# One sparse-attention stage in place of two: projection and compression merged, in 64x64 tiles, with the rope swap by SBUF transfers and all pages read by SyncE

## What is computed

```python
def nsa_project(h, w_in, pos):                       # h: 520 tokens x 1024
    z = h @ w_in                                     # 16 heads of q, six k/v groups of 4 x 64, gates
    ...
    return q, rope(q, pos), kc, vc, rope(ks, pos), vs, rope(kw, pos), vw, gates

def nsa_compress(k, pe, w):                          # blocks of 32 rows -> one row
    blk = k.reshape(B, L // L_CMP, L_CMP, NSA_KV, NSA_DH) + pe[:, None, :]
    return jnp.einsum('bclgd,lde->bcge', blk, w)

def nsa_compressed_select(q, kc, vc, pe, wc, qpos):
    kcmp = nsa_compress(kc, pe[0], wc[0])
    vcmp = nsa_compress(vc, pe[1], wc[1])
    ...
    s = jnp.einsum('btgjd,bcgd->bgjtc', qg, kcmp.astype(jnp.float32))   # scores of the compressed keys
    ...                                              # softmax, o_c, and by top_k the selected blocks
```

## Time and profile before

| | |
|---|---|
| time, median of 3 runs (lowest to highest) | 3682.13 us (3681.27 to 3682.18) |
| the profiled execution's own time | 3677.41 us |
| its span, mean granted TensorE clock | 3675.8 us, 0.943 |
| busy share: PE, DVE, ACT, POOL | 88%, 51%, 34%, 11% |
| sparse attention of layer 0, first projection matmul to first matmul of `nsa_attend` | 282.86 us |
| the same in layer 3 | 282.09 us |

### The profile page before, as it was taken

One profiled execution on the slowest core, in us unless ns is written; L12 is line 12 of the kernel. 1 busy time (PEld: TensorE's weight loads), 2 busy tenths in 40 slices (PEclk: granted clock), 3 DMA queues, 4 the chain that ended last, 5 costly groups with the idle time before them and its releaser, 6 DMA issues. The chain is left out here.

```text
span 3675.8 us, 65936 instructions
## 1 busy us (share of the span) xinstructions
PE 3239.0 (88%) x25906; PEld 2993.7 (81%) x25906; DVE 1870.1 (51%) x3122; ACT 1262.5 (34%) x2150; POOL 396.0 (11%) x313
## 2 busy tenths in 40 slices
PE   6966888999889787878999898999989768889997
PEld 6764568999889787758999887999976745789997
DVE  4113654636479745345636484645451136446363
ACT  2103553423245332124323383423231035434232
POOL 2111211000034100020000131000031112100000
PEclk9978999999999899789999998999999889999999
DMA  3163513222222000123222323222232644032222
GB/s 133 70 219 115 159 38 131 86 98 83 77 64 83 19 0 0 63 80 143 89 95 77 92 79 110 92 89 96 63 106 98 192 131 156 30 131 83 92 86 66
DMA packets 136924, 341.21 MB, mean 93 GB/s; under 512 B 42856, under 2 KB 89576, under 8 KB 122488
## 3 DMA queue, kind: packets, MB, share of 16 engines
q1 hardware_dynamic: 112376, 279.25, 23.4%
q0 software_dynamic: 10496, 46.15, 3.7%
q10 hardware_dynamic: 13824, 12.59, 1.1%
HBM read 322.60 MB, written 32.12 MB: 96 GB/s over the span
## 5 line engine op out<-in xcount | busy, mean ns | idle before, releaser
L354 PE MATMUL ffn_ps<-ffn_x_hi_sb,ffn_w_hi_sb 128*128 128x260 f32 x2816 | 572.0, 284 | 40.3 <-DVE ffn_x_lo_sb L165 37.1
L354 PE MATMUL ffn_ps<-ffn_x_hi_sb,ffn_w_lo_sb 128*128 128x260 f32 x2816 | 570.0, 284 | 0.0
L354 PE MATMUL ffn_ps<-ffn_x_lo_sb,ffn_w_hi_sb 128*128 128x260 f32 x2816 | 569.5, 284 | 0.0
L354 PEld LDWEIGHTS ffn_ps<-ffn_x_hi_sb,ffn_w_hi_sb 128*128 128x128 f32 x2816 | 437.1, 190 | 44.9 <-issue 35.8
L354 PEld LDWEIGHTS ffn_ps<-ffn_x_hi_sb,ffn_w_lo_sb 128*128 128x128 f32 x2816 | 437.0, 190 | 0.0
L354 PEld LDWEIGHTS ffn_ps<-ffn_x_lo_sb,ffn_w_hi_sb 128*128 128x128 f32 x2816 | 436.0, 190 | 0.0
L394 ACT ACTIVATE ffn_w_hi_sb<-ffn_raw_sb 128x2048 fp32r<-128x2048 f32 (+2 forms) x152 | 256.8, 1689 | 349.0 <-PE ffn_ps L354 349.0
L446 DVE TENSOR_TENSOR ffn_w_lo_sb<-ffn_raw_sb,ffn_w_hi_sb 128x2048 fp32r<-128x2048 f32 (+2 forms) x152 | 304.8, 2005 | 47.3 <-ACT ffn_w_hi_sb L394 47.3
L412 ACT ACTIVATE ffn_pre_sb<-ffn_ps 128x520 f32<-128x520 f32 x176 | 106.5, 605 | 605.8 <-PE ffn_ps L354 317.1
L461 DVE SCALAR_TENSOR_TENSOR ffn_conv_sb<-ffn_pre_sb,ffn_conv_w_sb,ffn_conv_sb 128x512 f32<-128x512 f32 x176 | 132.3, 752 | 345.1 <-ACT ffn_conv_sb L414 345.1
L354 PE MATMUL ffn_ps<-ffn_inner_hi_sb,ffn_w_hi_sb 128*128 128x260 f32 x1408 | 283.9, 283 | 6.5 <-DVE ffn_inner_lo_sb L479 3.4
(11 more groups left out here) (446 smaller groups left out, 6276.4 us busy)
## 6 DMA issues: line engine op xcount, KB each, us to landing
ffn_raw_sb<-ffn_w_in SPq DMA_DIRECT2D x88, 1024.0 KB, 4.9
ffn_raw_sb<-ffn_w_out SPq DMA_DIRECT2D x32, 768.0 KB, 4.2
nsae_ring_sb<-sel_pages SPq DMA_DIRECT2D x160, 128.0 KB, 2.2
ffn_raw_sb<-ffn_w_out SPq DMA_DIRECT2D x32, 640.0 KB, 3.9
nsap_w_raw_sb<-nsa_w_in SPq DMA_DIRECT2D x32, 512.0 KB, 3.7
gdnp_w_raw_sb<-gdn_w_in SPq DMA_DIRECT2D x32, 512.0 KB, 3.7
nsac_pages_sb<-cmp_pages ACTq DMA_DIRECT2D x96, 128.0 KB, 3.7
nsac_pages_sb<-cmp_pages SPq DMA_DIRECT2D x96, 128.0 KB, 3.6
```

Source lines behind the costliest of these rows:

```text
L354: mm = pe.matmul(psf[:, bank + h, 0:H], wp[:, w[0], w[1]:w[1] + P], xp[:, h * H:(h + 1) * H], start=start and k == 0, stop=stop and k == 2)
```

## The change

`nsa_project` and `nsa_compress` become one stage, `nsa_base` (buffers `nsab_`). Its parts:

- The 16 projection units are the same, in the order 8 to 15, 0 to 7.
- The rope swap is done by DMA: for each of the 12 turned units ACT issues four transfers of 8 partitions from SBUF to SBUF.
- The values and gates are projected in the split form: two passes of 280 columns, each eight steps (`v_step`) of 15 matmuls. Their weights pass through the same ring, which has two raw buffers in place of three.
- The compression is done in nine calls (the prompt, then each sample): 128 plain fp32 matmuls of 64x64 weights with 64 moving columns (40 for the prompt), over the four quadrants of the array; row group g2 writes PSUM bank 6+g2. The calls stand between projection units, and two of them between steps of the values.
- SP alone reads the pages, whole (256 KB, keys and values), four page numbers at a time; 64 transfers a layer.
- The prompt's scores are formed with the compressed keys as 32-column weights in four column tiles, and transposed afterwards.
- The 32 loads for `nsa_attend` are issued by SP after the last call; page numbers are read four at a time there too. Two stores of results are waited for at the end of `nsa_attend` in place of here.

```diff
-        w = Weights(sc, KT * P, 3, 2)
+        w = Weights(sc, KT * P, 2, 2)
...
-            def swap(r):
-                i = rotate[r]
-                pe.wait_ge(copied, i + 1)
...
-                for h in range(2):
-                    mm = pe.matmul(ps[:, 6 + h, 0:H], g.rope_swap, raw(i)[:, h * H:(h + 1) * H], start=True, stop=True)
...
-                    pe.matmul(ps[0:m, 2 * (i % 3), :], x, w_v[:, kt, 0:512], start=(kt == 0), stop=(kt == KT - 1))
-                    mm = pe.matmul(ps[0:m, 2 * (i % 3) + 1, 0:48], x, w_v[:, kt, 512:560], start=(kt == 0),
...
-                        mm = pe.matmul(ps[:, 1 + u % 2, gp * 256:gp * 256 + cols], w[:, kv, l, :], rhs,
-                                       start=(l == 0), stop=(l == 31))
...
+    order = [8, 9, 10, 11, 12, 13, 14, 15, 0, 1, 2, 3, 4, 5, 6, 7]
+    first_turn = 4
+    sample_after = {4: 0, 6: 1, 8: 2, 10: 3, 12: 4, 14: 5}
+    pages_after = {1: (0, 0), 2: (0, 1), 3: (1, 0), 4: (1, 1), 8: (2, 0), 9: (2, 1), 10: (3, 0), 11: (3, 1),
...
+                if b >= 2 and half == 0:
+                    sp.wait_ge(compressed, b)
...
+                _, ids = nc.values_load_multi_w_load_instructions(v.table[0:1, at:at + 4], engines=(sp.engine,),
...
+                if u in pages_after:
+                    pages(*pages_after[u])
...
+            sp.wait_ge(compressed, 9)
             for k in range(2):
-                sample_loads(sp, d, v, j, table, k, range(4), v.kv_in)
+                sample_loads(nc, sp, d, v, j, k, range(4), v.kv_in)
+            sp.wait_ge(v_copied, 10)
...
+                for l in range(32):
+                    for kv in range(2):
+                        for g2 in range(2):
+                            rows = slice(64 * g2, 64 * g2 + 64)
+                            to = 64 * (g2 if kv == 0 else 1 - g2)
+                            mm = pe.matmul(ps[to:to + 64, 6 + g2, 0:cols], w_cmp[rows, kv, l, :], views[rows, kv, l],
+                                           start=(l == 0), stop=(l == 31))
...
+                for tt in range(5):
+                    if kt == 0:
+                        pe.wait_ge(*((copied, 16) if p == 0 else (v_copied, tt + 1)))
...
+                    pe.matmul(out, x_hi[:, x], w_hi, start=(kt == 0), stop=False)
+                    pe.matmul(out, x_hi[:, x], w_lo, start=False, stop=False)
+                    mm = pe.matmul(out, x_lo[:, x], w_hi, start=False, stop=(kt == KT - 1))
...
+            v_step(0, 0)
+            c_scores(0)
+            v_step(0, 1), v_step(0, 2)
+            c_scores(1)
+            v_step(0, 3)
+            c_tokens(0)
+            v_step(0, 4)
+            compress_sample(6)
+            c_tokens(1)
+            for kt in range(5, KT):
+                v_step(0, kt)
+            for kt in range(0, 3):
+                v_step(1, kt)
+            compress_sample(7)
...
+                for base in (0, 64):
+                    for k in range(2):
+                        here, there = base + 8 * k, base + 8 - 8 * k
+                        act.dma_start(swap[here:here + 8, r % 2, :], raw(i)[there:there + 8, :]).then_inc(swapped[r % 2], 16)
```

More of the change, by code:

```diff
@@ new lines, in is_window, with landed, sample_loads @@
+def is_window(k):
+    return k % 6 >= 4
+def landed(k, pool):
+    loads = [m for m in range(k % 2, k + 1, 2) if m >= 2 or not pool]
+    return sum(16 * (1 if is_window(m) else 4) * (4 if m < 2 else 2) for m in loads)
+def sample_loads(nc, eng, d, v, j, k, strips, kv_in):
+    c, h, vals = k % 6 // 2, k % 2, k // 6
+    for l in strips:
+        slot = v.ring[:, k % 2 * 4 + l, :]
+        if is_window(k):
+            eng.dma_start(slot, d["win_state"][j, 4 * h + l, :, vals * 1024:(vals + 1) * 1024]).then_inc(kv_in[k % 2], 16)
+            continue
+        at = (4 * h + l) * PAGES + 4 * c
+        _, pages = nc.values_load_multi_w_load_instructions(v.table[0:1, at:at + 4], engines=(eng.engine,),
+                                                            min_val=0, max_val=N_PHYS - 1)
+        for p, page in enumerate(pages):
+            eng.dma_start(slot[:, p * 256:(p + 1) * 256],
+                          flat(d["sel_pages"][j, bass.ds(page, 1), :, vals * 256:(vals + 1) * 256]
+                               .rearrange("o p n -> p o n"))).then_inc(kv_in[k % 2], 16)
@@ L1522, in nsa_project @@
-        added = sc.sem("added")
+        swapped = [sc.sem(f"swapped{x}") for x in range(2)]
+        parted = sc.sem("parted")
         rotated = sc.sem("rotated")
[L1524 to L1545, removed]
@@ L1585, in _ @@
[L1585 to L1603, removed]
@@ L1605, in _ @@
[L1605 to L1624, removed]
@@ L1627, in nsa_compress @@
[L1627 to L1657, removed]
@@ L1665, in nsa_compress @@
+        c_masked = sc.sem("c_masked")
         c_shifted = sc.sem("c_shifted")
@@ L1680, in nsa_compress, with raw @@
         dve_own = sc.sem("dve_own")
+        stored = sc.sem("stored")
         block = ctx.enter_context(nc.Block())
[L1683 to L1695 removed]
+        def raw(i):
+            return v.qu[:, i, :] if i < 8 else (kv_c if i < 12 else v.kv)[:, i % 4, :]
@@ L1834, in _ @@
+            for x in (x_hi, x_lo):
+                ins = pool.memset(x[:, KT * N:].bitcast(F32), 0.0)
+            ins.then_inc(padded, 1)
+            w.rest(pool, 0)
+            pool.wait_ge(norm.summed, KT)
+            pool.memset(swap_flat, 0.0).then_inc(zeroed, 1)
+            for u in range(1, 22):
+                w.rest(pool, u)
         @block.vector
@@ L1904, in _ @@
             own.settle()
+            dve.wait_ge(v_copied, 5)
             for i in range(NCH):
```

675 lines of the change are left out of this document (397 added, 278 removed).

## The result

| | us, median (lowest to highest) |
|---|---|
| before, 4 runs | 3681.7 (3680.45 to 3682.18) |
| the change, 4 runs | 3560.26 (3557.67 to 3565.68) |

The ratio is 0.9673, with a 95% interval of 0.9656 to 0.9689: 121 us less. The forecast was 3517, 165 less, in a range of 3485 to 3600. The sign and the range held; the time lies outside the main case (3485 to 3545), and a quarter of the forecast gain is missing. The profiled execution of the change is the slowest of the four: 3565.68, span 3564.0, clock 0.945.

What follows compares the result with a forecast made beforehand. TensorE, busy 88% of the span, was taken as the bound, with two gaps (54 us a layer). Terms summed to 199.9 us against 282.86 and 282.09, saving 165.2 over two layers: 3517 us, range 3485 to 3600.

Steps and rivals of the forecast that it cites:

- main case: Whole kernel: the summed terms hold within their bounds, 3485 to 3545 us, chance 0.60.
- Tiles share a round: Compression calls: four quadrants of 64 columns run together, 58 ns a round, 3.7 us a call as lower bound.
- The swap's price: Projection: a rope swap costs TensorE 0.86 us; eleven leave the window, 103.60 to 94.1, a unit staying 5.77.
- The page gap: Before the compression: TensorE's 31.54 us standstill for a cached page goes, leaving pages at 0.
- The stall before the scores: Before the prompt's scores: TensorE newly waits 5.5 us for keys that VectorE makes after the last unit's rotation.
- the second pass of the values: Values: the second pass waits 2.4 us while ACT loads a function table and copies out the first's results.
- SP's tail: Stage end: SP's 32 loads after the last call take 30 us, plus 1.5 for stores and barrier.
- The rival of late weights or pages: Projection units: two-buffer ring or SP's single list delays loads, 3 us for each of 12 units, 3589; chance 0.10.
- nine calls at 4.5: Compression: nine calls of 128 matmuls (256 records) at 4.5 us each cost TensorE 40.5 us a layer.
- clock: 2: TensorE: short-tile stretch or stall may drop the clock to 1.2 GHz, costing 2 us a layer (0 to 4).
- the rival of a dearer record: Compression calls: the two row groups take turns, 28.8 ns a record, 7.4 us a call, 3569 in all; chance 0.15.
- The record that shares no round: Compression calls: tiles share no round, 57.5 ns a record, 15.0 us a call, 3706 in all, slower; chance 0.05.

## Why the prediction was right, and what it missed

**Right, with its mechanism.** Tiles share a round: 4.0 a call uninterrupted, for 3.7 to 4.5, and 7.58 when half of the quadrants are used. The swap's price: two units fill the time from 158.66, where one call ends, to 170.27, where the next starts, 5.8 each, and no wait names a transfer of the swap. The page gap is gone. The stall before the scores, forecast at 5.5, was 4.39, with 0.79 more for the last unit's copy; the second pass of the values waited 2.06 for 2.4. SP's tail was 30.1 for 31.5, with 14.12 of idle TensorE for about 16. The rival of late weights or pages fell: only the second unit waited for weights (1.67).

**The step that failed** is "nine calls at 4.5". The term had the array's time and nothing for bringing the instructions: 512 of them in 4.0 us, where before 256 filled 14.56 us without a pause. Pauses of 17.5 us in layer 0 are over half of the 31.8 by which the layer is longer than the sum. The second term that failed is "clock: 2": the work at the lower level cost some 16 by the estimate above, because it fell behind five of the eight pauses too, and not only at the stall or a short-tile stretch. With 2.3 of waits in the first units and 1.9 for the prompt's copies, which the sum did not have, less 0.5 for each call, 0.7 at the stall and the second pass and 1.4 at the tail, this makes 29 of the 31.8; the rest is open.

That the time fell into the range is luck: it lies above the main case, in the part that was there for a dearer record and for late loads, and neither came. It stands near the rival of a dearer record (3569), but for another reason than the one priced there: row groups don't take turns. (The record that shares no round was priced at 15.0 a call where 256 × 57.5 ns are 14.7, and the main case's lower bound, 3517 − 14 − 23, is 3480; neither bears on this.)

The Trainium skill has the two sides of this. "Runtime: NRT & Kernel Launch", section "Instruction fetch mechanics", says that instructions are brought in blocks of 16 KiB, 256 instructions, while the present one runs, and that this is mostly hidden. The traces agree with the block (28 packets more for 7136 records more) and not with the hiding in these calls. The floor of about 25 ns from the Trainium skill's "TensorE: Matmul & The Clock Gate", section "Wait — 56ns, not 53.3ns?", which the prediction weighed, does not hold across tiles: 15.8 ns a record were measured.

**Not priced at all:** the dropped wait for the norm. The first matmul stands 6.59 behind the norm in place of 13.57, but the first units then run into waits (0.30, 0.28 and 1.67) and half clock, and putting the wait back changed nothing. The prompt's copies held sample 0's call for 1.9.

**What stays open.** The two layers and the two earlier starts gain 116 us in the profiled execution, but its whole is only 112 below that of before; 3.1 of the difference lies in the DeltaNet layer, whose code is the same (from its norm's first matmul to that of the ConvFFN behind it, 675.69 for 672.62). The clock of the sparse-attention layers moved by several us between runs whose edits do not touch the calls, and what moves it was not tested; a few us between two kernels here can be that alone. That runs of the change spread over 8 us and those of before over 2 says little, as those of before spread over 10.5 beside the first experiments (3675.36 to 3685.89).

## What to carry to other kernels

When matmuls are cut smaller, price their instructions beside their columns: an engine that takes 256 instructions in 2 us can outrun what brings them, and the trace then shows pauses without a cause, at a fixed count of instructions and longer under DMA traffic. Spread such bursts between slower work, or give each instruction more columns; both gained some 50 us here (the second with half of the weight blocks left out). Price the clock with the pauses: by the estimate above the lower level cost TensorE some 10 us a layer more than before. And where an end is set by one engine's issue of transfers, an idle engine that takes half of them was worth 9 to 11 us a layer on top of the cheaper issue.

## What the runs showed of the hardware

- Four 64x64 tiles ran together: a round of four records took 4.0/64 = 62 ns for 64 columns of plain fp32, and 3.72/32 = 116 ns for 128. Fewer than 64 columns gained nothing: the prompt's records of 40 columns (203 in 3.22 us) took 63 ns a round.
- Stops of TensorE a multiple of 256 instructions apart, in the calls shown about 1.1 us without and 2.2 us with page traffic, where 512 instructions are used within 4 us; where 512 took 7.58 us, 16 of 18 calls had none.
- TensorE went on 1.25 to 1.62 us after a 16 KB instruction packet had landed, in all 18 such pauses; the packet itself took 0.87 to 1.15 us in the calls compared, with page traffic or without.
- A standstill of 2.31 us was followed by 3.4 us at 1.2 GHz; one of 2.52 us was not.
